# Softplus behind the index stage, x's second half behind the first weight unit, and sums of squares folded to one chunk

## The reference, cut to what matters

```python
def hybrid_layer(x, norm_g, w_in, ...):          # first block
    xn = rms_norm(x, norm_g)
    z = xn @ w_in
    ...
    h = rg_lru(causal_depthwise_conv(x_rnn, conv_w, conv_b), ..., lru_lambda)
    ...
    return x + mixed @ w_out

def rg_lru(x, w_a, b_a, w_x, b_x, lam):
    ...
    log_a = -LRU_C * r * jax.nn.softplus(-lam)    # lam: one value per channel, 1024 of them

# between the blocks: rms_norm(x, final_norm_gain), then in the second block
h = rmsnorm(x, attn_norm)                         # mean of squares over 1024 features
proj = h @ w_in                                   # gives c_q (768 wide), c_kv (256 wide), ...
q = rmsnorm(c_q, q_norm) @ w_uq                   # mean of squares over 768
kv = rmsnorm(c_kv, kv_norm) @ w_ukv               # mean of squares over 256
...                                               # attention, projection, 32 experts, final norm
```

## Time and profile before

| what | value |
|---|---|
| median of 3 runs | 712.9 us (712.58 to 713.73) |
| profiled execution: its own time | 713.73 us |
| its span in the trace | 711.9 us |
| busy: PE, DVE, ACT, POOL | 677.5, 328.9, 324.6, 378.7 us |
| chain that ended last | PE 87%, DMA 4%, DVE 4%, ACT 3% |

### The profile page before, as it was taken

How to read it: one execution, slowest core, us unless ns; L and a number is a source line. 1 busy time by engine, 2 the same in 40 slices (tenths; PEclk the granted TensorE clock), 3 DMA queues, 4 the chain that set the end, 5 groups by cost and what they waited for, 6 DMA issues and landing times.

```text
span 711.9 us, 14302 instructions
## 1 busy us (share of the span) xinstructions
PE 677.5 (95%) x5856; PEld 574.0 (81%) x5856; DVE 328.9 (46%) x672; ACT 324.6 (46%) x600; POOL 378.7 (53%) x284
## 2 busy tenths in 40 slices
PE   3999999999999999999999999999999999999793
PEld 3899899999999999998899999999665655555451
DVE  6869423787871347775754554433321212121102
ACT  7565677865553456664358664452211111111004
POOL 3978557798887989996697555881000000000000
PEclk9999999999999999999999999999999999999997
DMA  8845334434355555463447335799999999999992
GB/s 343 306 168 184 118 119 132 166 126 171 119 174 214 189 192 180 168 245 121 152 168 272 120 120 187 307 424 360 360 424 419 423 423 420 422 422 420 423 419 94
DMA packets 26131, 181.74 MB, mean 255 GB/s; under 512 B 2896, under 2 KB 3152, under 8 KB 4688
## 3 DMA queue, kind: packets, MB, share of 16 engines
q1 hardware_dynamic: 25488, 179.22, 65.0%
q10 hardware_dynamic: 576, 1.57, 0.7%
HBM read 179.73 MB, written 1.05 MB: 254 GB/s over the span
## 4 chain that ended last, share of the span: by engine, by line
PE 87%; DMA 4%; DVE 4%; ACT 3%; issue 1%; SPq 0%; ACTq 0%; DVEq 0%
PE D L466 49%; PE L L926 7%; PE L L905 7%; DMA scr<-w_expert_dram 4%; PE QB L959 4%; PE L L638 2%; PE D L990 2%; PE D L514 2%; PE TB L647 2%; PE TB L990 2%; PE L L610 1%; PE D L518 1%; DVE big_r L1506 1%; PE D L497 1%; PE OB L915 1%; PE QB L687 1%
## 5 line engine op out<-in xcount | busy, mean ns | idle before, releaser
L1489 POOL TENSOR_TENSOR ring_r<-ring,ring_r 128x512 fp32r<-128x512 f32 (+1 forms) x280 | 378.5, 1385 | 103.5 <-ACT ring_r L1076 103.3
L466 PE MATMUL D<-scr_r,ring_r 128*128 128x256 f32 x1104 | 214.0, 289 | 0.0
L1076 ACT ACTIVATE ring_r<-ring 128x1024 fp32r<-128x1024 f32 (+1 forms) x140 | 145.5, 1045 | 95.4 <-PE D L466 84.0
L466 PEld LDWEIGHTS D<-scr_r,ring_r 128*128 128x128 f32 x1104 | 175.6, 191 | 2.4 <-issue 1.3
L466 PE MATMUL D<-hT_r,ring_r 128*128 128x256 f32 x552 | 156.1, 283 | 0.0
L466 PE MATMUL D<-big_r,ring_r 128*128 128x256 f32 x1110 | 137.2, 284 | 0.0
L466 PEld LDWEIGHTS D<-big_r,ring_r 128*128 128x128 f32 x1110 | 134.3, 192 | 1.7 <-issue 1.0
L466 PEld LDWEIGHTS D<-hT_r,ring_r 128*128 128x128 f32 x552 | 105.7, 192 | 1.1 <-issue 0.7
L905 PEld LDWEIGHTS L<-wkr,big 128*128 128x128 f32 x496 | 56.6, 192 | 11.2 <-issue 11.2
L1506 DVE SCALAR_TENSOR_TENSOR th<-th,L 64x256 f32<-64x256 f32 x32 | 13.4, 418 | 104.3 <-ACT th L1411 103.7
L905 PE MATMUL L<-wkr,big 128*128 128x64 f32 x496 | 58.6, 276 | 0.5 <-DVE wkr L1922 0.5
(11 more groups left out here) (380 smaller groups left out, 996.4 us busy)
## 6 DMA issues: line engine op xcount, KB each, us to landing
ring<-w_dense_dram SPq DMA_DIRECT2D x69, 1024.0 KB, 4.9
big<-w_expert_dram SPq DMA_DIRECT2D x38, 1024.0 KB, 21.0
ring<-w_expert_dram SPq DMA_DIRECT2D x24, 1024.0 KB, 19.4
wu<-w_expert_dram SPq DMA_DIRECT2D x5, 1024.0 KB, 16.8
small<-w_expert_dram SPq DMA_DIRECT2D x5, 1024.0 KB, 16.9
scr<-w_expert_dram SPq DMA_DIRECT2D x5, 1024.0 KB, 19.9
hT<-w_expert_dram SPq DMA_DIRECT2D x5, 1024.0 KB, 22.0
attn<-w_expert_dram SPq DMA_DIRECT2D x5, 1024.0 KB, 17.4
```

The source lines that it names most:

```text
L466: last = mm(out_, r32(w[i][ws]), r32(x[j][xs_]), start=start and m == 0, stop=stop and m == 2)
L1076: A_(r32(hi_unit(j)[w]), dense_unit(j)[w], ACT.Copy).then_inc(hi_ready, 1)
L1489: last = g.tensor_tensor(r32(w), w, r32(h).bitcast(F32), ALU.subtract)
```

## The change

1. Softplus: both ACT steps move from the start into the q stage (behind `q_in(0)` and behind `v1_in(1)`), and the log takes its added 1 as a bias. VectorE's ten steps move behind the convolution, which follows the index stage.
2. The second half of x moves from ACT's queue to SP's, behind the first unit and ahead of the second. ACT waits for `vec` itself.
3. `fold` is followed by `fold_pair`, which adds the last two chunks, so every sum over partitions takes one matmul. c_q gets two folds and a pair add, c_kv a pair add. TensorE waits for `folded` in all four places.

```diff
@@ sync @@
-            for h in range(2):
-                sp_.dma_start(dense_unit(h), w_dense[0][:, h * UNIT:(h + 1) * UNIT]).then_inc(arrived[0] if h else s_in["first_unit"], 16)
+            sp_.dma_start(dense_unit(0), w_dense[0][:, 0:UNIT]).then_inc(s_in["first_unit"], 16)
+            sp_.dma_start(xT[:, 4:8, :], x_half(1)).then_inc(s_in["x1"], 16)
+            sp_.dma_start(dense_unit(1), w_dense[0][:, UNIT:2 * UNIT]).then_inc(arrived[0], 16)
@@ tensor @@
             def sum_folded(n, dst, src):
 
                 pe.wait_ge(folded, n - N_FIN1 + 1)
-                for c in range(2):
-                    last = mm(dst[:, 0:T], ones, src[:, c, :], start=(c == 0), stop=(c == 1))
-                last.then_inc(ssq, 1)
+                mm(dst[:, 0:T], ones, src[:, 0, :], start=True, stop=True).then_inc(ssq, 1)
...
-            sumsq(N_CQ, src=cq_sq)
+            pe.wait_ge(rooted, N_CQ)
+            sum_folded(N_CQ, UB, cq_sq)
             for c in range(4):
                 chunk("kb", c, h2)
                 if c == 0:
-                    sumsq(N_CKV2, src=ck_sq)
+                    pe.wait_ge(rooted, N_CKV2)
+                    sum_folded(N_CKV2, UB, ck_sq)
@@ scalar @@
-            for h in range(2):
-                act.dma_start(xT[:, 4 * h:4 * h + 4, :], x_t[:, 4 * h * T:4 * (h + 1) * T].rearrange(
-                    "p (c t) -> p c t", c=4)).then_inc(s_in[f"x{h}"], 16)
-            act.wait_ge(sp_step, 2)
-            A_(sp[:, 2, :], sp[:, 1, :], ACT.Exp, scale=-1.0).then_inc(sp_act, 1)
-            act.wait_ge(sp_step, 3)
-            A_(sp[:, 4, :], sp[:, 3, :], ACT.Ln).then_inc(sp_act, 1)
+            act.dma_start(xT[:, 0:4, :], x_half(0)).then_inc(s_in["x0"], 16)
+            act.wait_ge(s_in["vec"], 16)
...
             q_in(0)
+            act.wait_ge(sp_step, 2)
+            A_(sp[:, 2, :], sp[:, 1, :], ACT.Exp, scale=-1.0).then_inc(sp_act, 1)
             v1_in(0)
             q_in(1)
             v1_in(1)
+            act.wait_ge(sp_act, 1)
+            A_(sp[:, 4, :], sp[:, 2, :], ACT.Ln, bias=1.0).then_inc(sp_act, 1)
             v1_in(2)
@@ vector @@
             def fold(src, i, ready):
 
                 dve.wait_ge(sq, ready)
-                ins = v.tensor_tensor(src[:, 0:2, :], src[:, 0:2, :], src[:, 2 * i:2 * i + 2, :], ALU.add)
-                ins.then_inc(folded, 1) if i == 3 else step(ins)
+                step(v.tensor_tensor(src[:, 0:2, :], src[:, 0:2, :], src[:, 2 * i:2 * i + 2, :], ALU.add))
+
+            def fold_pair(src):
+
+                v.tensor_tensor(src[:, 0, :], src[:, 0, :], src[:, 1, :], ALU.add).then_inc(folded, 1)
...
             for half, squared in enumerate((scr, hT)):
                 for i in (2, 3):
                     fold(squared, i, SQ0[N_FIN1] + 2 * i + 1 + half)
+                fold_pair(squared)
...
+            for i in (1, 2):
+                fold(cq_sq, i, SQ0[N_CQ] + i + 1)
+            fold_pair(cq_sq)
+            dve.wait_ge(sq, SQ0[N_CKV2] + 1)
+            fold_pair(ck_sq)
             kept(dve, "ckv2", 0)
             raw_mean(N_CQ)
```

More of the change, by code:

```diff
@@ L361, in x1_src, with x_half @@
             return src
+        def x_half(h):
+            return x_t[:, 4 * h * T:4 * (h + 1) * T].rearrange("p (c t) -> p c t", c=4)
         block = ctx.enter_context(nc.Block())
@@ L873, in _ @@
                     route(c // 2 - 1)
-            pe.wait_ge(folded, 3)
+            pe.wait_ge(folded, 5)
             sum_tokens(0)
@@ L1540, in _ @@
             v.memset(xr[:, :, 0:CONV], 0.0).then_inc(padded, 1)
[L1541 to L1554, removed]
             for c in range(DC):
@@ L1623, in _ @@
                 ins.then_inc(conv_done, 1)
+            dve.wait_ge(sp_act, 2)
+            step(v.tensor_scalar(sp[:, 3, :], sp[:, 2, :], 1.0, None, ALU.add))
+            step(v.tensor_scalar(sp[:, 5, :], sp[:, 3, :], 1.0, None, ALU.is_equal))
+            step(stt(sp[:, 6, :], sp[:, 3, :], -1.0, sp[:, 5, :], ALU.add, ALU.add))
+            step(v.reciprocal(sp[:, 7, :], sp[:, 6, :]))
+            step(v.tensor_tensor(sp[:, 6, :], sp[:, 4, :], sp[:, 5, :], ALU.add))
+            step(v.tensor_tensor(sp[:, 6, :], sp[:, 6, :], sp[:, 2, :], ALU.mult))
+            step(v.tensor_tensor(sp[:, 6, :], sp[:, 6, :], sp[:, 7, :], ALU.mult))
+            step(stt(sp[:, 6, :], sp[:, 0, :], 0.0, sp[:, 6, :], ALU.max, ALU.add))
+            step(v.tensor_scalar(sp[:, 7, :], sp[:, 6, :], LRU_C / 2, None, ALU.mult))
+            v.tensor_scalar(sp[:, 8, :], sp[:, 6, :], -LRU_C / 2, None, ALU.mult).then_inc(sp_ready, 1)
             def bias_max(a):
```

## The result

The changed kernel takes 718.28 us (median of 13 runs, 716.62 to 722.09); the kernel before, on the same chip, 713.8. The ratio is 1.0052, 95% interval [1.0034, 1.007], or 3.7 us (2.4 to 5.0); the two medians lie 4.5 us apart. It is slower. The profiled execution took 718.74 us with a span of 716.9, 5.0 more than before.

A forecast was written before the change was run, and what follows sets the result against it. TensorE was taken to bound the kernel. Start -0.15, FIN1 and ATT2 +1.4, c_q +1.7, c_kv -0.43 and clock +1.3 gave +3.8 us on 712.9, so 716.7 us, range 712.2 to 717.8.

The forecast's parts named there:

- What bounds the kernel: TensorE bounds the whole kernel; what it gains or loses before 350 us passes to the end in full.
- The start: ACT's first table load and rounding of x begin slightly sooner: -0.15 us, bounds -0.6 and +0.1.
- Softplus: At its new places ACT's loads and VectorE's ten steps (estimated 2 us) fit into idle time: zero.
- FIN1 and ATT2: Sums at N_FIN1 and N_ATT2: pair adds beside GpSimd make TensorE wait 0.5 and 1.5 us, together +1.4.
- The sum of c_q: Six matmuls become one, but TensorE waits 3.8 us for folds beside busy GpSimd: +1.7 us.
- c_kv: Its pair add is done before TensorE wants it, so its sum saves 0.43 us.
- The clock: TensorE's clock falls after the 3.8 us wait at c_q: +1.3 us, between 0 and 1.6.
- rival 5: At the start, a drain behind the table load: +3.8 + 1.35, 718.0 us; chance 0.03.
- rival 2: VectorE's adds at the sums slip between GpSimd's ops: 2.8 us less, 710.1 us; chance 0.10.
- rival 3: GpSimd partly idle during c_q's folds, so only the first place costs: about 712.9 us; chance 0.12.
- rival 4: VectorE's delay also makes chunk_pair("qb") wait, or the clock falls twice: +5.5, 718.4 us; chance 0.08.

The follow-up runs named there:

- all sums in time, once more: The all sums in time kernel measured a second time, without making GpSimd take turns: 711.81 us, 0.9964 of the kernel before.
- quiet GpSimd: Changed kernel, but GpSimd writes zeros in place of its subtraction for the four units of kb: 715.25 us, 1.0012 of the kernel before.
- the sums alone: Kernel before with only the four new sums, softplus and queues untouched: 718.63 us, 1.006 of the kernel before.
- the table load first: Changed kernel with a one-column ACT copy ahead of its wait for x: 718.39 us, 1.0052 of the kernel before.
- FIN1 and ATT2 from two chunks: Changed kernel with those two sums as before, c_q and c_kv as changed: 716.71 us, 1.0029 of the kernel before.
- all sums in time: Changed kernel, FIN1 and ATT2 from two chunks, c_q/c_kv adds before xT scaling, wkr split and wrt scaling after c_kv's mean: 711.78 us, 0.9959 of kernel before.

## Why the prediction was right, and where its terms were off

The forecast was +3.8 us and 716.7 us. Measured were +3.7 us by the ratio, +4.5 by the medians of 13 runs each (718.28 and 713.8), and +5.0 in the profiled pair. The ratio on the forecast's own 712.9 gives 716.6; the median of 718.28 itself lies above the range's 717.8, as the kernel before was 0.9 us above the 712.9 in these runs. The agreement to 0.1 us is in part luck: in the profile the start gave more than its term and the clock took more. By its own steps:

- **What bounds the kernel.** Right in the profiled pair: each microsecond that TensorE lost before 330 us was there at the end (+4.92 became +5.0).
- **The start,** -0.15. Mis-sized in the profiles: -0.5 to -0.6, the lower bound. x's half landed 0.3 us sooner, which the term had held fixed ("The half's own landing should not move"). In another profile of the same start (all sums in time, once more) x's half landed at 5.93 and the first matmul came at 10.09, later than before, so the landing varies by more than the term. The drain was not there. That the panel's landing would be the start's next limit, the working had not seen.
- **Softplus,** 0. Right: two loads in ACT's idle time. VectorE's ten steps took 4.0 us, twice the estimate, and nobody waited.
- **FIN1 and ATT2,** +1.4 with waits of 0.5 and 1.6. Right: +1.5, waits 0.6 and 1.2. Carrying GpSimd's ops forward one by one was worth it.
- **The sum of c_q,** +1.7 with a wait of 3.8. Right: +1.6 and 3.7, and 3.8 in three more kernels. The quiet GpSimd shows the cause: without its reads the four adds are 4 us shorter, VectorE's two instructions ahead of them 2.1 us, and there is no wait. That VectorE comes to the adds late is the other half: done early, they are in time beside the same GpSimd.
- **c_kv,** -0.43. Right.
- **The clock,** +1.3, between 0 and 1.6. Right that it falls; too small for this profile, which shows 2.8 us. The bound came from one fall of 3.41 us; here it lasted 6.83, over the sum and most of the 24 matmuls behind it. It isn't so in every execution. Four profiles have the unfilled wait of 3.7 to 3.8 us at c_q. In two (the changed kernel, the sums alone) the fall lasted 6.83 us and cost 2.8; in the other two (the table load first, FIN1 and ATT2 from two chunks) it lasted 3.41 and cost 1.7 and 1.6, which is the term's bound. What decides between the two is open. The times fit this: five of the 13 runs had a mean clock of 0.987 or 0.988 and a median of 718.5, the other eight, at 0.990 and above, 717.0. But a mean clock doesn't say where the fall was, so that the eight had the shorter one at c_q isn't shown. The working also read its row a little wrong: the 0.81 us of idle time and the 0.58 are of the same window (676 to 680 us), and the fall began at 676.64.

Quick adds (rival 2) and the half (rival 3) fall with the waits. Of the delay that reaches further (rival 4, 718.4, closer to the median of 718.28 than the forecast) one half came: a fall of the clock twice as long. The other, a wait for qb, didn't: TensorE was idle for 5.62 us from 280 to 330, and the three waits at the sums are all of it. The drain (rival 5) is out with the rows of the start.

## What to carry to other kernels

Matmuls that a faster sum saves are worth 0.43 us each here, while an add that TensorE waits for costs up to its own length beside GpSimd, 1.4 to 1.7 us; so move adds to VectorE only where they end before TensorE comes, and look in the order at what stands ahead of them. Here c_q's adds, 8 us earlier and with the router's weights behind them, and without the two adds at FIN1 and ATT2, turned 0.5% slower into 0.4% faster. A wait of TensorE of some microseconds should be priced with the clock behind it (here 1.6 to 2.8 us behind a wait of 3.7 to 3.8), and one profile isn't enough for that price: another execution may hold a fall of half the length, or one at another place.

## What the runs showed of the hardware

**A subtraction can be shut out.** In three of the thirteen profiles (the quiet GpSimd, FIN1 and ATT2 from two chunks, all sums in time) VectorE's first subtraction of `hT` lasted 10.4 us, begun 0.10 to 0.23 us behind one of GpSimd's; in those in which it lasted 1.2 to 1.8 us it had begun 0.08 to 0.66 behind. So that distance alone doesn't decide it, and what does is open. The Trainium skill says that issue order decides who blocks, for the whole instruction (SBUF — State Buffer, Who interferes with whom); these rows show that the one that blocks can hold on for seven instructions more.

**A small instruction with one input waits too.** VectorE's and GpSimd's timelines of the changed kernel:
```profile
80.63 1.14 DVE L1625 TENSOR_SCALAR sp<-sp 128x8 f32<-128x8 f32 x1
81.80 1.20 DVE L1626 TENSOR_SCALAR sp<-sp 128x8 f32<-128x8 f32 x1
...
80.43 3.80 POOL L1493 TENSOR_TENSOR ring_r<-ring,ring_r 128x512 fp32r<-128x512 f32 x3 [3.92 <-ACT ring_r L1081]
```
Eight columns took 0.17 us while GpSimd was idle, and 1.14 and 1.20 under its subtractions, each until that op's end.
